# Stage openings of a 24-stage network kernel: remainders of the first PSUM bank ahead of units 3 and 4, for the lower token half too

## Chip, cores and metric

One core of a Trainium2 chip. The metric is device microseconds of one execution. A run's time is that of the whole program; three runs were taken.

## What is computed

Two blocks of four layers each on 256 tokens of width 1024 (float32, batch 1). The first block has, per layer, a gated FFN, a mixer (a spatial gate, dilated window attention or forgetting attention, each with attention over a memory) and a second FFN. The second has a mixer (block sparse attention, stick-breaking attention, a convolution, MoBA) and a squared-ReLU MLP per layer.

```
x = x + 0.5 * rms_norm(swiglu_ffn(rms_norm(x, g[0]), ...), g[1])
h = rms_norm(x, g[2])
y = mixer_a | mixer_b | mixer_c (h, rms_norm(mem), ...)
x = x + rms_norm(y, g[3])
x = x + 0.5 * rms_norm(swiglu_ffn(rms_norm(x, g[4]), ...), g[5])
...
x = x + mixer(_rms_norm(x, attn_norm[i]))
hm = _rms_norm(x, mlp_norm[i])
x = x + jnp.square(jax.nn.relu(hm @ mlp_w_up[i])) @ mlp_w_down[i]
```

Every stage thus starts with a norm of x and a product of the result with a weight matrix. Where these meet is what the change is about.

## The kernel before

**Stages.** The program is one list: four times ffn, mem_kv, mixer, ffn, then four times mixer (nsa, stick, conv, moba) and mlp. All but mem_kv begin with an *opening*, so there are 20. The 256 tokens are two halves of 128, lower (t = 0) and upper (t = 1).

**Products in three parts.** A float32 operand is written as a rounded part (hi) and the remainder (lo), and a product is hi*hi + hi*lo + lo*hi. In `half_chunk` on TensorE (PE) `hi_products` (L799, L800) multiplies the activations' hi with the weights' hi and lo, and `lo_product` (L803) the activations' remainder act_lo with the weights' hi.

**Weights.** They come in *units* of two 128-row tiles by up to 512 columns through a ring of 8 slots (SyncE issues the loads). Four units, numbered 0 to 3 here, make a chunk (K = 1024); units 4 to 7 are the next. ScalarE (ACT) copies a landed unit to ring_hi (L1402), then VectorE (DVE) subtracts it to get ring_lo (L1915, "split" below); the semaphores are hi_ready and lo_ready, in order of units. For stages that follow neither mem_kv nor the start, GpSimd (POOL) does the splits of units 5 and 7 (L2757, pool_lo_ready) instead. How far DVE splits ahead is given by the calls of `ahead(limit)` that are spread over its program.

**Activations.** In an opening PE transposes the normed rows nrm of a half, 8 tiles into two PSUM banks T0 and T1 (L775). DVE multiplies each bank with the gain into act_hi (L1929, two instructions of 128x512), then computes act_lo tile by tile (L1939, four instructions per bank, out = T * gain - act_hi); the last one of a bank raises t_taken of that bank. The generator `normed` holds these instructions, and the callers draw them with `next`: `start` for the lower half, in the midst of the residual of the stage before, and the stage's own code for the upper half. After `start` DVE updates x for the upper half of the previous stage (L2090 and L2093, or L2097), which its norm waits for.

**PE's order in an opening** (`opening`, `half_chunk` with lo_later): the first chunk takes the hi products first and the remainders later. Lower half: units 0 to 3, then a wait for both banks, then all eight remainder products. Upper half: units 0 and 1, a wait for bank 0, four remainder products, units 2 and 3, a wait for bank 1, the other four. Then follows the second chunk of the same half (units 4 to 7, all three parts together), and then the other half.

## Time and profile before

| | |
|---|---|
| runs | 3346.24 (median), 3345.96, 3359.56 us |
| profiled execution | 3356.01 us, its span 3354.3 us |
| PE matmul busy | 96% of the span |
| DVE busy | 58% |
| ACT busy | 49% |
| POOL busy | 6% |
| granted TensorE clock | 0.99 on average |
| chain that ended last | PE 86%, DVE 9%, ACT 3% |

The profile is of one execution. The span runs from the first to the last instruction. Busy shares are the union of an engine's instructions; PE's instructions overlap and their ends are modelled, so the start of each is what to go by. Idle time of an engine is put down to what released it. An instruction of DVE that has started also counts as busy while it waits for a port.

### The profile page before, as it was taken

The numbers are of one execution on the slowest core, as the hardware profiler recorded it, in microseconds if no ns is written. First come the engines' busy times: TensorE is split into PE (matmuls) and PEld (weight loads), VectorE is DVE, ScalarE is ACT, GpSimd is POOL, SyncE is SP. The second block draws the span as 40 slices with busy tenths as digits, with TensorE's granted clock in tenths as the row PEclk, the third lists the DMA queues.
The fourth block names the chain that finished last, engine by engine and source line by source line (L and its number), as shares of the span: only waits on it lengthen the run. The fifth ranks groups of instructions, "written<-read, shape, count | busy, mean of one in ns | idle before, by whom it ended". The sixth has DMA issues, their size and how long they took to land.

```text
span 3354.3 us, 52004 instructions
## 1 busy us (share of the span) xinstructions
PE 3227.4 (96%) x19601; PEld 2822.5 (84%) x19601; DVE 1933.2 (58%) x2856; ACT 1627.4 (49%) x2425; POOL 199.0 (6%) x258
## 2 busy tenths in 40 slices
PE   7999999998999999999999999899999999999999
PEld 7977988977998978897987897779788887887797
DVE  4656546565555654655556556565466566655663
ACT  4445445444444435544445445544354455545552
POOL 1001001000001000101000102000000000102100
PEclk9999999999999999999999999999999999999999
DMA  6653656642565643565554654435544550555364
GB/s 218 194 176 123 200 182 189 200 151 89 169 194 175 194 155 117 157 192 178 185 186 146 182 184 150 135 113 187 181 135 154 187 181 13 187 183 170 112 202 150
DMA packets 413278, 551.69 MB, mean 164 GB/s; under 512 B 33952, under 2 KB 263520, under 8 KB 413104
## 3 DMA queue, kind: packets, MB, share of 16 engines
q1 hardware_dynamic: 409248, 536.10, 49.8%
q0 software_dynamic: 2864, 10.38, 1.0%
q10 hardware_dynamic: 992, 2.84, 0.2%
q8 instruction: 114, 1.87, 0.2%
q14 instruction: 60, 0.49, 0.0%
HBM read 548.15 MB, written 1.05 MB: 164 GB/s over the span
## 4 chain that ended last, share of the span: by engine, by line
PE 86%; DVE 9%; ACT 3%; issue 1%; POOL 0%; DMA 0%; SPq 0%; DVEq 0%; ACTq 0%
PE G L799 15%; PE G L803 15%; PE G L800 15%; PE G L900 11%; PE G L901 11%; PE G L902 11%; DVE ring_lo_sb L1915 4%; PE T L775 2%; PE S L994 1%; PE O L1022 1%; DVE act_hi_sb L1929 1%; DVE act_lo_sb L1939 1%; PE G L1302 1%; ACT ring_hi_sb L1402 1%; DVE work_sb L2116 0%
## 5 line engine op out<-in xcount | busy, mean ns | idle before, releaser
L1915 DVE TENSOR_TENSOR ring_lo_sb<-ring_sb,ring_hi_sb 128x1024 fp32r<-128x1024 f32 (+1 forms) x998 | 1200.9, 1222 | 610.8 <-ACT ring_hi_sb L1402 592.4
L1402 ACT ACTIVATE ring_hi_sb<-ring_sb 128x1024 fp32r<-128x1024 f32 (+1 forms) x1028 | 1056.0, 1044 | 681.1 <-DMA ring_sb<-ffn_w_down 217.0
L900 PE MATMUL G<-act_hi_sb,ring_hi_sb 128*128 128x256 f32 x3136 | 877.1, 280 | 3.0 <-DVE ring_lo_sb L1915 3.0
L901 PE MATMUL G<-act_lo_sb,ring_hi_sb 128*128 128x256 f32 x3136 | 874.2, 279 | 0.0
L902 PE MATMUL G<-act_hi_sb,ring_lo_sb 128*128 128x256 f32 x3136 | 873.5, 279 | 0.0
L799 PE MATMUL G<-ring_hi_sb,hid_hi_sb 128*128 128x512 f32 x1456 | 582.5, 400 | 13.8 <-DVE hid_hi_sb L1948 6.5
L900 PEld LDWEIGHTS G<-act_hi_sb,ring_hi_sb 128*128 128x128 f32 x3136 | 589.5, 188 | 3.4 <-issue 3.2
L902 PEld LDWEIGHTS G<-act_hi_sb,ring_lo_sb 128*128 128x128 f32 x3136 | 589.1, 188 | 0.0
L901 PEld LDWEIGHTS G<-act_lo_sb,ring_hi_sb 128*128 128x128 f32 x3136 | 588.7, 188 | 0.0
L800 PE MATMUL G<-ring_lo_sb,hid_hi_sb 128*128 128x512 f32 x1456 | 578.5, 397 | 0.0
L803 PE MATMUL G<-ring_hi_sb,hid_lo_sb 128*128 128x512 f32 x1248 | 493.2, 395 | 0.0
L799 PE MATMUL G<-ring_hi_sb,act_hi_sb 128*128 128x512 f32 (+2 forms) x960 | 386.0, 402 | 36.2 <-DVE ring_lo_sb L1915 23.2
L800 PE MATMUL G<-ring_lo_sb,act_hi_sb 128*128 128x512 f32 (+2 forms) x960 | 371.5, 387 | 0.0
L799 PEld LDWEIGHTS G<-ring_hi_sb,hid_hi_sb 128*128 128x128 f32 x1456 | 275.3, 189 | 83.0 <-DVE hid_hi_sb L1948 8.2
L803 PE MATMUL G<-ring_hi_sb,act_lo_sb 128*128 128x512 f32 (+2 forms) x960 | 326.0, 383 | 8.7 <-DVE act_lo_sb L1939 8.7
L800 PEld LDWEIGHTS G<-ring_lo_sb,hid_hi_sb 128*128 128x128 f32 x1456 | 275.4, 189 | 65.1
L1988 DVE TENSOR_TENSOR work_sb<-G,work_sb 128x256 f32<-128x256 f32 (+1 forms) x240 | 117.1, 492 | 364.6 <-ACT work_sb L1453 364.6
L1453 ACT ACTIVATE work_sb<-G 128x256 f32<-128x256 f32 (+1 forms) x120 | 52.9, 441 | 513.6 <-PE G L902 412.3
L803 PEld LDWEIGHTS G<-ring_hi_sb,hid_lo_sb 128*128 128x128 f32 x1248 | 234.4, 188 | 57.7
L799 PEld LDWEIGHTS G<-ring_hi_sb,act_hi_sb 128*128 128x128 f32 x960 | 183.6, 191 | 99.4 <-DVE ring_lo_sb L1915 34.7
L803 PEld LDWEIGHTS G<-ring_hi_sb,act_lo_sb 128*128 128x128 f32 x960 | 179.9, 188 | 51.0 <-issue 13.6
L800 PEld LDWEIGHTS G<-ring_lo_sb,act_hi_sb 128*128 128x128 f32 x960 | 184.2, 192 | 34.0
(264 smaller groups left out, 2608.9 us busy)
## 6 DMA issues: line engine op xcount, KB each, us to landing
ring_sb<-ffn_w_gate_up SPq DMA_DIRECT2D x704, 256.0 KB, 3.9
ring_sb<-ffn_w_down SPq DMA_DIRECT2D x352, 256.0 KB, 3.7
ring_sb<-mlp_w_up SPq DMA_DIRECT2D x256, 256.0 KB, 3.6
ring_sb<-mlp_w_down SPq DMA_DIRECT2D x256, 256.0 KB, 3.7
ring_sb<-a_w_in SPq DMA_DIRECT2D x48, 256.0 KB, 4.3
ring_sb<-sb_w_in SPq DMA_DIRECT2D x48, 256.0 KB, 3.9
ring_sb<-moba_w_in SPq DMA_DIRECT2D x48, 256.0 KB, 4.1
ring_sb<-w_mem_kv SPq DMA_DIRECT2D x32, 256.0 KB, 3.8
```

The lines of the kernel that those rows point to most:

```text
L775: last = nc.tensor.transpose(bank[0:m, at:at + P], src, ident)
L799: mm(dst, lhs[0][:, kt, ts], ring_hi[:, slot, k, 0:w], start=start, stop=False)
L800: mm(dst, lhs[0][:, kt, ts], ring_lo[:, slot, k, 0:w], start=False, stop=False)
L803: return mm(dst, lhs[1][:, kt, ts], ring_hi[:, slot, k, 0:w], start=False, stop=stop)
L900: mm(dst, hi, act_hi[:, kt, :], start=(kt == 0 and f == 0), stop=False, skip_group_check=True)
L901: mm(dst, hi, act_lo[:, kt, :], start=False, stop=False, skip_group_check=True)
L902: last = mm(dst, lo, act_hi[:, kt, :], start=False, stop=(kt == KT - 1), skip_group_check=True)
L994: last = mm(S[:, t, 0:w], q, keys, start=(t == 0), stop=True, skip_group_check=True)
L1402: fn(ring_hi[:, s_, :, 0:w], ring[:, s_, :, 0:w], ACT.Copy).then_inc(hi_ready, 1)
L1453: fn(gated[:, par, 1, 0:w], G[:, 1, par, 0:w], f).then_inc(gated_ready, 1)
L1915: v.tensor_tensor(ring_lo[:, s_, :, 0:w], ring[:, s_, :, 0:w], ring_hi[:, s_, :, 0:w], ALU.subtract).then_inc(lo_ready, 1)
L1988: v.tensor_tensor(hid[:, par, t, 0:w], G[:, t, par, lo:lo + w], gated[:, par, t, 0:w], ALU.mult).then_inc(g_taken[t], 1)
```

## The change

For the lower half PE now does what it did for the upper one: after units 0 and 1 it waits for bank 0 and multiplies that bank's four remainders, and only then waits for unit 2's split and the second act_hi. On DVE the generator `normed` has one more stop, between the act_lo of bank 0 and that of bank 1. `start` draws act_hi and the act_lo of bank 0, then splits up to unit 3, then draws the act_lo of bank 1. All other callers draw three times in a row, which is the order they had. Line numbers of what follows move up by three for PE's part.

```diff
--- before.py
+++ after.py
@@ -818,13 +818,12 @@
                     return last
                 for u in range(CHUNK_UNITS):
                     slot = (n + u) % RING
+                    if lo_later and u == half:
+                        copied(c["T"] - 2)
+                        remainders(0, half)
+                        pe.wait_ge(act_hi_in, c["act_hi"])
                     if t == 0:
                         unit_split(n + u, step, i)
-                    if lo_later and u == half:
-                        if t == TT - 1:
-                            copied(c["T"] - 2)
-                            remainders(0, half)
-                        pe.wait_ge(act_hi_in, c["act_hi"])
                     for k in range(UNIT_K):
                         kt = UNIT_K * u + k
                         hi_products(dst, lhs, kt, ts, slot, k, width, kt == 0)
@@ -833,10 +832,8 @@
                     if t == TT - 1 and not lo_later:
                         last.then_inc(unit_used, 1)
                 if lo_later:
-                    if t == 0:
-                        copied(c["T"] - 2)
                     copied(c["T"] - 1)
-                    last = remainders(0 if t == 0 else half, CHUNK_UNITS)
+                    last = remainders(half, CHUNK_UNITS)
                 if t == 0:
                     last.then_inc(first_done, 1)
 
@@ -1932,6 +1929,8 @@
                             .then_inc(act_hi_in, 1)
                     yield
                     for b in range(2):
+                        if b:
+                            yield
                         n = c["T"]
                         dve.wait_ge(act_hi_in, c.up("act_hi"))
                         for j in range(4):
@@ -1956,8 +1955,8 @@
                 ahead(c["unit"] + CHUNK_UNITS)
                 if before is not None:
                     ahead(c["unit"] + RING)
-                    next(before)
-                    next(before)
+                    for _ in range(3):
+                        next(before)
                 for d, (c0, w) in enumerate(plan_):
                     c.up("unit", CHUNK_UNITS)
                     for t in range(TT):
@@ -2013,8 +2012,8 @@
                         split_one(n + d * CHUNK_UNITS + u, step, i)
 
                 ahead(n + RING)
-                next(before)
-                next(before)
+                for _ in range(3):
+                    next(before)
                 tb, turn0 = c["T"], c["turn"]
                 one(0, 0)
                 split_chunk(2)
@@ -2068,6 +2067,7 @@
                 if s < len(stages) and stages[s][0] != "mem_kv":
                     started[s] = normed(s)
                     next(started[s])
+                    next(started[s])
                     ahead(c["unit"] + CHUNK_UNITS)
                     next(started[s])
                 ahead(c["unit"] + CHUNK_UNITS + 1)
@@ -2146,8 +2146,8 @@
                 lead, cut, _ = quanta(kind)
                 before = started.pop(s)
                 ahead(n + RING)
-                next(before)
-                next(before)
+                for _ in range(3):
+                    next(before)
 
                 def take(d, t):
                     if t == 0:
@@ -2574,8 +2574,8 @@
                     done()
 
                 ahead(n + RING)
-                next(before)
-                next(before)
+                for _ in range(3):
+                    next(before)
                 tb = c["T"]
                 product(0, 0)
                 product(0, 1)
```

The stick stage's opening, lower half, on DVE: act_hi and act_lo are the activations' two parts, ring_lo a split, x_sb<-G the residual. Before:

```order
L1929 TENSOR_TENSOR act_hi_sb<-T,an_cols_sb 128x4x128 x2
L1915 TENSOR_TENSOR ring_lo_sb<-ring_sb,ring_hi_sb 128x1024 x2
L1939 SCALAR_TENSOR_TENSOR act_lo_sb<-T,an_cols_sb,act_hi_sb 128x128 x8
L1915 TENSOR_TENSOR ring_lo_sb<-ring_sb,ring_hi_sb 128x1024
L2097 TENSOR_TENSOR x_sb<-G,x_sb 128x1024
L1915 TENSOR_TENSOR ring_lo_sb<-ring_sb,ring_hi_sb 128x1024
```

With the change:

```order
L1926 TENSOR_TENSOR act_hi_sb<-T,an_cols_sb 128x4x128 x2
L1938 SCALAR_TENSOR_TENSOR act_lo_sb<-T,an_cols_sb,act_hi_sb 128x128 x4
L1912 TENSOR_TENSOR ring_lo_sb<-ring_sb,ring_hi_sb 128x1024 x2
L1938 SCALAR_TENSOR_TENSOR act_lo_sb<-T,an_cols_sb,act_hi_sb 128x128 x4
L1912 TENSOR_TENSOR ring_lo_sb<-ring_sb,ring_hi_sb 128x1024
L2097 TENSOR_TENSOR x_sb<-G,x_sb 128x1024
L1912 TENSOR_TENSOR ring_lo_sb<-ring_sb,ring_hi_sb 128x1024
```

The first four act_lo have moved ahead of the two splits (units 2 and 3). In the first opening and the four after mem_kv it is four and three splits, in the three ffn that follow an ffn and in nsa one, and in the other seven none.

The same opening on PE, from the first product on; t_taken0 and t_taken1 stand for the act_lo of the two banks. Before, from unit 2 on:

```order
L799 MATMUL G<-ring_hi_sb,act_hi_sb 128x512 [waits act_hi_in,lo_ready]
L800 MATMUL G<-ring_lo_sb,act_hi_sb 128x512
L799 MATMUL G<-ring_hi_sb,act_hi_sb 128x512
L800 MATMUL G<-ring_lo_sb,act_hi_sb 128x512
L799 MATMUL G<-ring_hi_sb,act_hi_sb 128x512 [waits lo_ready]
L800 MATMUL G<-ring_lo_sb,act_hi_sb 128x512
L799 MATMUL G<-ring_hi_sb,act_hi_sb 128x512
L800 MATMUL G<-ring_lo_sb,act_hi_sb 128x512
L803 MATMUL G<-ring_hi_sb,act_lo_sb 128x512 [waits t_taken1,t_taken0]
L803 MATMUL G<-ring_hi_sb,act_lo_sb 128x512 x7
```

With the change, from the end of unit 1 on:

```order
L803 MATMUL G<-ring_hi_sb,act_lo_sb 128x512 [waits t_taken0]
L803 MATMUL G<-ring_hi_sb,act_lo_sb 128x512 x3
L799 MATMUL G<-ring_hi_sb,act_hi_sb 128x512 [waits lo_ready,act_hi_in]
L800 MATMUL G<-ring_lo_sb,act_hi_sb 128x512
L799 MATMUL G<-ring_hi_sb,act_hi_sb 128x512
L800 MATMUL G<-ring_lo_sb,act_hi_sb 128x512
L799 MATMUL G<-ring_hi_sb,act_hi_sb 128x512 [waits lo_ready]
L800 MATMUL G<-ring_lo_sb,act_hi_sb 128x512
L799 MATMUL G<-ring_hi_sb,act_hi_sb 128x512
L800 MATMUL G<-ring_lo_sb,act_hi_sb 128x512
L803 MATMUL G<-ring_hi_sb,act_lo_sb 128x512 [waits t_taken1]
L803 MATMUL G<-ring_hi_sb,act_lo_sb 128x512 x3
```

The remainder products are now two groups of four, each with its own bank's wait, and the waits for unit 2 and for the second act_hi stand behind the first group.

## Rows read from the trace of the kernel before

**Rows 1.** Waits view: engine, line, releaser: us in total, times, longest.
```profile
PE G L799 <- DVE ring_lo_sb L1915: 23.2, 21, 2.8
PE G L803 <- DVE act_lo_sb L1939: 8.7, 9, 1.0
```

**Rows 2.** Timeline of DVE, stick opening: start us, us, instruction, count, [idle before].
```profile
2400.90 1.29 DVE L1929 TENSOR_TENSOR act_hi_sb<-T,an_cols_sb 128x512 fp32r<-128x512 f32 x2 [7.62 <-PE T L775]
2402.10 2.35 DVE L1915 TENSOR_TENSOR ring_lo_sb<-ring_sb,ring_hi_sb 128x1024 fp32r<-128x1024 f32 x2
2404.37 2.16 DVE L1939 SCALAR_TENSOR_TENSOR act_lo_sb<-T,an_cols_sb,act_hi_sb 128x128 fp32r<-128x128 f32 x8
2406.44 1.35 DVE L1915 TENSOR_TENSOR ring_lo_sb<-ring_sb,ring_hi_sb 128x1024 fp32r<-128x1024 f32 x1
2407.72 1.21 DVE L2097 TENSOR_TENSOR x_sb<-G,x_sb 128x1024 f32<-128x1024 f32 x1
2409.15 2.00 DVE L1915 TENSOR_TENSOR ring_lo_sb<-ring_sb,ring_hi_sb 128x1024 fp32r<-128x1024 f32 x1 [0.22 <-DVE x_sb L2097]
```

**Rows 3.** Timeline of PE, the same opening.
```profile
2401.64 0.50 PE L799 MATMUL G<-ring_hi_sb,act_hi_sb 128*128 128x512 f32 x1 [0.35 <-DVE act_hi_sb L1929]
...
2406.67 2.10 PE L803 MATMUL G<-ring_hi_sb,act_lo_sb 128*128 128x512 f32 x8 [0.97 <-DVE act_lo_sb L1939]
...
2414.21 1.04 PE L775 MATMUL T<-con_sb,nrm_sb 128*128 128x128 f32 x8
```

**Rows 4.** Timelines of ACT (two rows) and POOL (two), the same opening.
```profile
2402.86 1.06 ACT L1402 ACTIVATE ring_hi_sb<-ring_sb 128x1024 fp32r<-128x1024 f32 x1 [0.22 <-DMA ring_sb<-sb_w_in]
2411.87 1.15 ACT L1423 ACTIVATE nrm_sb<-x_sb,small_sb 128x1024 f32<-128x1024 f32 x1 [1.76 <-POOL small_sb L2718]
...
2403.99 2.72 POOL L2757 TENSOR_TENSOR ring_lo_sb<-ring_sb,ring_hi_sb 128x1024 fp32r<-128x1024 f32 x1 [8.62 <-ACT ring_hi_sb L1402]
2406.66 3.40 POOL L2757 TENSOR_TENSOR ring_lo_sb<-ring_sb,ring_hi_sb 128x1024 fp32r<-128x1024 f32 x1
```

**Rows 5.** Timelines of DVE (two rows) and POOL (one), opening of nsa.
```profile
2045.12 1.29 DVE L1929 TENSOR_TENSOR act_hi_sb<-T,an_cols_sb 128x512 fp32r<-128x512 f32 x2 [0.75 <-PE T L775]
...
2049.55 2.13 DVE L1915 TENSOR_TENSOR ring_lo_sb<-ring_sb,ring_hi_sb 128x1024 fp32r<-128x1024 f32 x1
...
2048.19 2.41 POOL L2757 TENSOR_TENSOR ring_lo_sb<-ring_sb,ring_hi_sb 128x1024 fp32r<-128x1024 f32 x1 [0.22 <-ACT ring_hi_sb L1402]
```

**Rows 6.** Timelines of DVE (two rows) and PE (one), opening after first mem_kv.
```profile
225.89 1.28 DVE L1929 TENSOR_TENSOR act_hi_sb<-T,pre_cols_sb 128x512 fp32r<-128x512 f32 x2
...
232.56 5.28 DVE L1915 TENSOR_TENSOR ring_lo_sb<-ring_sb,ring_hi_sb 128x1024 fp32r<-128x1024 f32 x4
...
232.79 0.70 PE L803 MATMUL G<-ring_hi_sb,act_lo_sb 128*128 128x512 f32 x2 [0.96 <-DVE act_lo_sb L1939]
```

**Rows 7.** Timeline of PE, the first opening.
```profile
14.31 0.77 PE L799 MATMUL G<-ring_hi_sb,act_hi_sb 128*128 128x512 f32 x1 [2.01 <-DVE ring_lo_sb L1915]
...
17.43 0.63 PE L800 MATMUL G<-ring_lo_sb,act_hi_sb 128*128 128x512 f32 x1
...
22.45 2.10 PE L803 MATMUL G<-ring_hi_sb,act_lo_sb 128*128 128x512 f32 x8 [0.96 <-DVE act_lo_sb L1939]
```

**Rows 8.** Timelines of DVE and POOL: first opening, then the moba stage.
```profile
12.95 2.35 DVE L1915 TENSOR_TENSOR ring_lo_sb<-ring_sb,ring_hi_sb 128x1024 fp32r<-128x1024 f32 x2
13.74 0.47 POOL L2711 TENSOR_SCALAR pool_tmp_sb<-sums_sb 128x1 f32<-128x1 f32 x1 [4.71 <-ACT nrm_sb L1413]
...
3062.46 0.42 DVE L2304 TENSOR_TENSOR head_tmp_sb<-proj_sb,tabs_sb 128x256 f32<-128x256 f32 x1
3061.70 1.27 POOL L2716 TENSOR_SCALAR head_rs_sb<-pool_neg_sb 128x4 f32<-128x4 f32 x1
```

**Rows 9.** Timelines of DVE and POOL, opening of conv.
```profile
2712.72 0.69 DVE L1929 TENSOR_TENSOR act_hi_sb<-T,an_cols_sb 128x512 fp32r<-128x512 f32 x1 [7.62 <-PE T L775]
2716.04 2.48 POOL L2757 TENSOR_TENSOR ring_lo_sb<-ring_sb,ring_hi_sb 128x1024 fp32r<-128x1024 f32 x1 [8.84 <-ACT ring_hi_sb L1402]
```

## Prediction

> **What bounds the kernel now.** I read the page's busy shares first: TensorE (PE) is busy for 96% of the span (the table above), VectorE (DVE) for 58%, so some 4% is left in which PE stands still. So a change in order can only pay where PE stands still, and the waits view says what ends those stretches. Two rows of it belong to the stage openings: 8.7 us, in nine waits, for the activation remainders (act_lo, L1939), and 23.2 us, in 21 waits, for weight remainders (ring_lo, L1915) [rows 1]. The first is what the change can remove; the second is what it can add to, since it moves act_lo ahead of ring_lo on DVE.
>
> Then I read one opening on each engine. Times from here on are counted from the start of the first act_hi write of the opening, 2400.90 in the stick stage. DVE: two act_hi writes, weight splits of units 2 and 3 from 1.20 to 3.55, eight act_lo from 3.47 to 5.63, split of unit 4 until 6.89, the x update (L2097) until 8.03, split of unit 6 from 8.25 to 10.25 [rows 2]. PE: first product at 0.74, remainders only at 5.77 after 0.97 idle, upper half's transposes at 13.31 [rows 3]. Between the last two lie 8 + 24 = 32 matmuls, so one is 0.235 us. POOL does units 5 and 7: the first starts at 3.09, 0.07 after ScalarE's (ACT) copy of unit 5 [rows 4].
>
> The third thing to see is in durations. A POOL split that meets nothing takes 2.4 [rows 5], a DVE split 1.2 (two in 2.35, rows 2). But POOL's first of this opening takes 2.72: it started while DVE was in the split of unit 3, and ended 2.26 after that one. DVE's split of unit 6 takes 2.00, and ends 1.09 after POOL's second [rows 2, 4]; in the nsa stage's opening DVE's split of unit 4 takes 2.13, and ends 1.08 after POOL's first [rows 5]. So a DVE split and a POOL split exclude each other, and the later waits for all that is left. The act_lo writes (one operand in PSUM) pass beside POOL at their usual 0.26 each.
>
> **The change, part by part.** There are 20 openings. Instructions are neither added nor removed. PE does four of its eight remainder products after unit 1; DVE does the four act_lo of bank 0 ahead of the splits up to unit 3. Every such split comes 4 x 0.26 = 1.04 later, what follows the eight act_lo keeps its place on DVE unless POOL shifts it.
>
> (a) Seven openings without a DVE split between act_hi and act_lo: DVE's order is the same, PE had no wait for act_lo. Nothing.
>
> (b) Four openings after mem_kv. POOL does no splits there. DVE goes through three splits and then act_lo; PE's remainders start at 232.79, which is 6.90 after zero, and end at 8.78 [rows 6]. Now: act_lo of bank 0 until 2.33, splits until 3.46, 4.60, 5.73, act_lo of bank 1 until 6.75 as before. PE: unit 0 from 0.74, unit 1 from 3.52, four remainders from 4.56, unit 2 from 5.5, unit 3 from 6.4, remainders from 7.4 to 8.3. Gain 0.48 each. In the first one DVE's four splits behind act_lo take 5.28 [rows 6] instead of the 4.6 of four undisturbed ones (the first is held until 8.55), and that takes 0.3 back: together 1.6. PE is the engine that all wait for until the upper half, so this reaches the end.
>
> (c) The very first opening. Splits 0 and 1 come 1.04 later, 2 and 3 wait for ACT's copies as before, act_lo ends 1.04 earlier. PE's eight remainders start at 22.45 and end at 24.3 [rows 7]; now the last four can start at 21.4. PE has units 0 and 1 a microsecond late, and they run at half speed there (eight products from 14.31 to 17.9, rows 7): unit 0 from 15.3, unit 1 from 17.1, four remainders from 18.9, unit 2 from 19.8, unit 3 from 20.7, remainders from 21.7 to 22.6. Gain 1.7.
>
> (d) Four openings with one DVE split in between (the three ffn that follow an ffn, and nsa). PE doesn't wait for act_lo there, but later, for DVE's split of unit 6 at the end of a gapless DVE chain (part of the 23.2 us in rows 1). So what PE has done earlier is of no use. That chain moves only where POOL's first split is asked for before DVE's of unit 3 has ended: in the nsa stage it started at 3.07 after zero [rows 5], now DVE's split lasts until 3.46. Loss 0.2 once.
>
> (e) Four openings with two DVE splits in between: stick, conv, moba, and the mlp after conv. Here the remainder wait is a full 0.97, and here DVE now has two splits back to back at 2.24 to 4.6, just where POOL asks for the port (3.09 in rows 4, between 2.7 and 3.3 in the others). Who gets it between the two? The trace has the case small. In the first opening POOL's one-column L2711 starts during the first of two back-to-back splits, and ends at 14.21, 0.13 after the second has begun (14.08): it was let in between them [rows 8]. Against that stands L2716 of the moba stage, which was let in only after the last of three rope products, and ended 0.09 after it [rows 8]; but those three have no semaphore wait between them, and splits do. I take the first. Then: split 2 until 3.46; POOL's first from 3.32 to 5.70; DVE's split 3 until 5.70 + 1.08 = 6.78; act_lo of bank 1 until 7.82; POOL's second until 6.78 + 2.27 = 9.05; split 4 until 10.13; x until 11.26; split 6 until 12.70. PE: unit 2 from 3.55 to 4.49; unit 3 from 6.84 to 7.88; remainders from 7.97 to 9.0; unit 4 from 10.19 to 11.7; unit 5 until 13.1, 6 and 7 until 15.9, where the transposes stood at 13.31. Loss 2.6. Late next would be the upper half's nrm: x at 11.26 instead of 8.03 makes it 15.4 at the latest (12.12 before, rows 4), still ahead of PE. In the conv stage POOL asks at 3.32 [rows 9], exactly at the hand-over; if DVE goes through, POOL's first ends at 6.83, split 4 at 7.91, split 6 at 11.26, PE's transposes at 14.2: loss 0.9. I take that one for conv.
>
> Sum: 3 x 2.6 + 0.9 + 0.2 - 1.6 - 1.7 = **+5.6 us**. The profiled execution took 3356.01 (span 3354.3), some 10 above the median of 3346.24 of the three runs, so I add the sum to the median: 3351.8.
>
> A rule bears on the one open point. By the trace the conv stage is a toss. The Trainium skill (SBUF — State Buffer, § Who interferes with whom) says that an operation of DVE with two SBUF inputs and one of GpSimd that reads SBUF exclude each other, and that whoever issues first has the port for its whole instruction. The durations of rows 2, 4 and 5 agree. By that rule POOL, which issues at 3.32 in conv against DVE's 3.37, would get it there too.
>
> **Rivals.**
> 1. POOL goes first in all four, the conv stage included: 1.7 more, 3353.5. For it: POOL's start at 3.32 is ahead of 3.37. Against: how long after its start it asks for the port no row shows. It is the outcome of the skill's rule above.
> 2. DVE keeps the port over both splits, as over the rope products: 4 x 0.9 + 0.2 - 3.3 = +0.5, 3346.7. For it the three rope products; against it L2711.
> 3. The port costs nothing new, because POOL is put off without harm: then (e) gains only 0.14 each, since split 6 at 10.25 holds PE 2.5 later: 4 x 0.14 + 3.3 = 3.9 less, 3342.4. Against: POOL's second split and split 6 follow each other in rows 2 and 4.
> 4. TensorE's clock falls in the new 2.35 us of idle at unit 3. After 2.0 idle, and a longer one before, the products from 14.31 on stand 0.43 to 0.45 apart instead of 0.235 [rows 7]; after shorter ones (0.97 in rows 3) they don't. At half speed until unit 4's work is through it would cost another 1.3 in each of three or four: 3355.7 to 3358.7.
> 5. **Slower than before by what can be measured**: POOL takes the port ahead of unit 3's split in the openings (d) as well, eight in all at 2.6: 20.8 - 3.3 = +17.5, 3363.7. It decides once POOL's first split starts before DVE's of unit 3 is through its predecessor, at 2.2; the earliest there is 3.07 [rows 5], as ACT's copy of unit 5 ends only then. Transfers would have to land 0.8 earlier.
> 6. The reordering does nothing that can be seen, gains and losses being swallowed by later waits: 3346.
>
> **How the numbers follow.** My case 0.35, rival 1 0.20, rival 2 0.20, rival 3 0.10, rival 4 0.08, rival 5 0.03, rival 6 0.04. A measurement of this kernel can tell about 0.5%, 16.7 us, from no change. All cases but rival 5 lie within that, so: faster 0.02 (rival 3 with what spread the runs have), same 0.93, slower 0.05 (rival 5, and rival 4 with that spread; one of the three runs shown is 13 above the others). The range goes from rival 3 to rival 4, 3341.5 to 3358.5. Its ends also hold the bounds of the two unknown prices: the port in (e), from 4 x 0.14 gained to 4 x 3.9 lost, and (c), from nothing to 1.9 gained.
>
> **What would show it.** In the changed profile: the nine waits of L803 for act_lo fall from 8.7 us to near nothing; in the stick, moba and post-conv mlp openings DVE's second split after the first four act_lo takes about 3.4 instead of 1.2, and PE has a new wait for ring_lo of about 2.3 there and one of 1.2 at unit 4, with the upper half's transposes at 15.9 after zero; in the nsa opening the wait for unit 6 is 0.2 longer. If DVE's two splits take 1.2 each there and POOL's first takes 3.7, rival 2 is right; if PE's products after the new idle are 0.43 apart, rival 4. The forecast is wrong in kind if those openings get shorter than before, or if the four openings after mem_kv don't.

## Result: 0.31% slower, and where it was lost

| | before | after |
|---|---|---|
| runs | 3358.80 us (median of 20) | 3369.84 us (median of 20) |
| lowest | 3345.96 | 3357.17 |
| ratio of after to before | | 1.0031, 95% interval 1.0020 to 1.0042 |
| profiled execution, its span | 3356.01, 3354.3 | 3369.36, 3367.6 |
| PE, DVE, ACT, POOL busy | 96, 58, 49, 6% | 96, 58, 48, 6% |

The ratio is worth +10.4 us (0.0031 x 3358.8), 6.7 to 14.1 by its interval. That is less than the 0.5% which the forecast took as the least that can be told from no change, but the interval lies wholly above 1. The forecast was +5.6 us, 3351.8, with a range up to 3358.5. One of the 20 runs of the changed kernel took 7944.59 us, for a reason that isn't known, and is left out of the ratio.

The waits view of the changed kernel, its three largest rows, the first of which answers to [rows 1] (engine, line, releaser: us in total, times, longest):

```profile
PE G L799 <- DVE ring_lo_sb L1912: 40.1, 30, 3.0
PE T L775 <- ACT nrm_sb L1420: 26.2, 6, 11.0
PE G L799 <- DVE act_hi_sb L1926: 12.5, 34, 0.5
```

There is no row for act_lo any more: the 8.7 us that the change went for are gone. But the wait for weight remainders has grown from 23.2 to 40.1 us. So 8.7 went and 16.9 came.

The stick opening on DVE, to be laid beside [rows 2] (start us, us, instruction, count, [idle before]); zero is 2400.35 here:

```profile
2400.35 1.29 DVE L1926 TENSOR_TENSOR act_hi_sb<-T,an_cols_sb 128x512 fp32r<-128x512 f32 x2 [7.61 <-PE T L775]
2401.56 1.12 DVE L1938 SCALAR_TENSOR_TENSOR act_lo_sb<-T,an_cols_sb,act_hi_sb 128x128 fp32r<-128x128 f32 x4
2402.59 4.54 DVE L1912 TENSOR_TENSOR ring_lo_sb<-ring_sb,ring_hi_sb 128x1024 fp32r<-128x1024 f32 x2
2407.05 1.12 DVE L1938 SCALAR_TENSOR_TENSOR act_lo_sb<-T,an_cols_sb,act_hi_sb 128x128 fp32r<-128x128 f32 x4
2408.09 2.35 DVE L1912 TENSOR_TENSOR ring_lo_sb<-ring_sb,ring_hi_sb 128x1024 fp32r<-128x1024 f32 x1
2410.37 1.21 DVE L2097 TENSOR_TENSOR x_sb<-G,x_sb 128x1024 f32<-128x1024 f32 x1
2411.80 1.23 DVE L1912 TENSOR_TENSOR ring_lo_sb<-ring_sb,ring_hi_sb 128x1024 fp32r<-128x1024 f32 x1 [0.22 <-DVE x_sb L2097]
```

Two weight splits in a row take 4.54 us where they took 2.35 [rows 2]. POOL's two run between 2403.40 and 2409.36:

```profile
2403.40 5.96 POOL L2757 TENSOR_TENSOR ring_lo_sb<-ring_sb,ring_hi_sb 128x1024 fp32r<-128x1024 f32 x2 [8.57 <-ACT ring_hi_sb L1399]
```

Taken singly, DVE's splits run 2.24 to 3.46 and 3.37 to 6.78 after zero, POOL's 3.05 to 5.69 and 5.65 to 9.01. So POOL was let in between DVE's two, DVE's second ended 1.09 after POOL's first, and POOL's second 2.23 after that one. PE in the same opening (to be laid beside [rows 3]):

```profile
2403.07 1.10 PE L803 MATMUL G<-ring_hi_sb,act_lo_sb 128*128 128x512 f32 x4
...
2407.19 0.50 PE L799 MATMUL G<-ring_hi_sb,act_hi_sb 128*128 128x512 f32 x1 [2.07 <-DVE ring_lo_sb L1912]
2407.52 0.58 PE L800 MATMUL G<-ring_lo_sb,act_hi_sb 128*128 128x512 f32 x1
2407.90 0.63 PE L799 MATMUL G<-ring_hi_sb,act_hi_sb 128*128 128x512 f32 x1
2408.33 0.63 PE L800 MATMUL G<-ring_lo_sb,act_hi_sb 128*128 128x512 f32 x1
2408.75 1.91 PE L803 MATMUL G<-ring_hi_sb,act_lo_sb 128*128 128x512 f32 x4
...
2416.45 1.03 PE L775 MATMUL T<-con_sb,nrm_sb 128*128 128x128 f32 x8
```

The remainders of bank 0 now run without idle time before them. After unit 2's products PE stands still until unit 3's split is there, at 6.84, and the upper half's transposes start at 16.09 after zero instead of 13.31.

That last number, the start of the upper half's transposes after zero, is the yardstick of all that follows, since it holds one opening and nothing else. It has a spread of its own: in the version below that changes (e) alone, the first opening, which that version leaves as it was, came 0.90 longer than before, and others came up to 0.99 shorter. So in single openings differences below 1 us count only where they come again in several versions, or where the rows show their cause. The 20 openings by the prediction's groups, after less before, in us:

| group | forecast | measured | single openings |
|---|---|---|---|
| (a) seven without a DVE split between | 0 | +1.85 | +1.29, +0.38, -0.04, +0.08, -0.14, +0.18, +0.10 |
| (b) four after mem_kv | -1.6 | -0.61 | +0.26, -0.58, -0.58, +0.29 |
| (c) first opening | -1.7 | -0.82 | |
| (d) three ffn after an ffn, nsa | +0.2 | +0.42 | +0.79, -0.32, -0.30, +0.25 |
| (e) stick, conv, mlp after conv, moba | +8.7 | +10.66 | +2.78, +2.64, +2.62, +2.62 |
| sum | +5.6 | +11.50 | |

The sum of +11.5 agrees with the +10.4 of the runs. The two spans differ by 13.3, so 1.8 lie outside the openings.

### The profile page after: what moved, and what is told of

It is laid out like the page before. It is cut to its first block, busy times and chain, and to the rows that moved or that the text cites. A ratio compares the mean times of both kernels' runs of the same rounds, so it can differ in the third digit from the quotient of the medians.

```text
span 3367.6 us, 51984 instructions
## 1 busy us (share of the span) xinstructions
PE 3231.8 (96%) x19601; PEld 2830.7 (84%) x19601; DVE 1945.0 (58%) x2856; ACT 1627.4 (48%) x2425; POOL 193.0 (6%) x258
## 4 chain that ended last, share of the span: by engine, by line
PE 86%; DVE 8%; ACT 3%; issue 1%; DMA 0%; POOL 0%; DVEq 0%; ACTq 0%; SPq 0%
PE G L799 16%; PE G L803 15%; PE G L800 15%; PE G L897 11%; PE G L898 11%; PE G L899 11%; DVE ring_lo_sb L1912 4%; PE T L775 2%; PE O L1019 1%; PE S L991 1%; DVE act_hi_sb L1926 1%; PE G L1299 1%; ACT ring_hi_sb L1399 1%; DVE act_lo_sb L1938 1%; DVE work_sb L2116 0%
## 5 line engine op out<-in xcount | busy, mean ns | idle before, releaser
L799 PE MATMUL G<-ring_hi_sb,act_hi_sb 128*128 128x512 f32 (+2 forms) x960 | 388.7, 405 | 52.8 <-DVE ring_lo_sb L1912 40.1
L803 PE MATMUL G<-ring_hi_sb,act_lo_sb 128*128 128x512 f32 (+2 forms) x960 | 333.1, 388 | 0.0
```

The lines of the kernel that those rows point to most:

```text
L799: mm(dst, lhs[0][:, kt, ts], ring_hi[:, slot, k, 0:w], start=start, stop=False)
L803: return mm(dst, lhs[1][:, kt, ts], ring_hi[:, slot, k, 0:w], start=False, stop=stop)
```

## Experiments

All ratios are against the kernel before, run on the same chip in turns. There were three such series on three chips, so compare ratios, not microseconds, between versions of different series; the medians of before in them were 3355.55, 3358.29 and 3357.31. Line numbers in the variants are up to 15 higher. Stages 18, 20, 21 and 22 of the program are those of (e). The variants share one addition: two sets of stages that say where DVE draws bank 0's act_lo early (NEW_DVE) and where PE takes bank 0's remainders early (NEW_PE).

```diff
--- after.py
+++ variants
+        NEW_DVE, NEW_PE = ..., ...
...
-                    if lo_later and u == half:
+                    early = lo_later and (t == TT - 1 or n in new_pe_units)
+                    if early and u == half:
                         copied(c["T"] - 2)
                         remainders(0, half)
+                    if lo_later and u == half:
                         pe.wait_ge(act_hi_in, c["act_hi"])
...
-                    next(started[s])
+                    if s in NEW_DVE:
+                        next(started[s])
                     ahead(c["unit"] + CHUNK_UNITS)
                     next(started[s])
+                    if s not in NEW_DVE:
+                        next(started[s])
```

### The change everywhere but in (e), and in (e) alone

```diff
+        NEW_DVE, NEW_PE = ALL - {18, 20, 21, 22}, ALL - {18, 20, 21, 22}
```

> The change everywhere but in the four openings with two splits (stick, conv, the mlp after conv, moba), which keep the old order on both engines. If the port hold-up in those four is the whole loss, their upper-half transposes stand at 13.3 us after the first act_hi again, and the kernel is 1 to 2 us faster than before (ratio 0.9995, not to be told from 1 by the times alone). If the loss is spread over other stages or comes from more half-clock stretches, the ratio stays above 1.001.

```diff
+        NEW_DVE, NEW_PE = {18, 20, 21, 22}, {18, 20, 21, 22}
```

> Only those four openings in the new order, all other 16 as before. Port theory: transposes at 15.95 to 16.1 in each (2.6 to 2.8 later), together +10.7 us, ratio 1.003. Spread theory: under half of that, ratio under 1.0015.

Without (e): 0.9992, interval 0.9976 to 1.0007, 3353.73 us. (e) alone: 1.0021, 1.0005 to 1.0037, 3362.91. So the loss is in (e), whose four openings stand at 13.31 to 13.51 again in the first version, and what the rest of the change gives can't be told from nothing.

In three of the four openings (e) alone costs +2.63, +2.64 and +2.63, as in the whole change. In moba it costs +0.92, and that one shows the mechanism from the other side. DVE and POOL there (zero is 3049.05):

```profile
3051.29 2.35 DVE L1920 TENSOR_TENSOR ring_lo_sb<-ring_sb,ring_hi_sb 128x1024 fp32r<-128x1024 f32 x2
3053.56 1.12 DVE L1946 SCALAR_TENSOR_TENSOR act_lo_sb<-T,an_cols_sb,act_hi_sb 128x128 fp32r<-128x128 f32 x4
3054.60 2.39 DVE L1920 TENSOR_TENSOR ring_lo_sb<-ring_sb,ring_hi_sb 128x1024 fp32r<-128x1024 f32 x1
...
3052.75 6.50 POOL L2768 TENSOR_TENSOR ring_lo_sb<-ring_sb,ring_hi_sb 128x1024 fp32r<-128x1024 f32 x2 [9.22 <-ACT ring_hi_sb L1407]
```

POOL's first split began at 3.70, behind DVE's second at 3.37, and DVE's two took their 2.35. POOL had to wait instead, its first took 3.16 (to 6.86), and what was held was DVE's split of unit 4 (2.39 instead of 1.2) and of unit 6. So DVE's order is the same in both cases, and POOL's start, 3.27 or earlier against 3.70, decides between 2.6 and 0.9.

### No POOL splits at all, in the new order and in the old

DVE splits every unit. First with the change everywhere, then in the old order.

```diff
-                by_pool |= {n + 5, n + 7}
+                by_pool |= set()
...
-                c.up("finished", 2)
+                c.up("finished", 0)
```

> The change, and DVE does the splits of units 5 and 7 as well, POOL none. Port theory: DVE's second split takes 1.2 again instead of 3.4, unit 3 no longer waits, transposes of the four openings within 0.3 us of those of the same kernel in the old order. Rival (the act_lo moved ahead cost the time by themselves, 1.04 us each, passed on through DVE's chain): transposes at least 1 us later than in the old order without POOL.

> The order before, POOL does no splits: the partner of the run above. DVE's chain gets two splits longer in the openings with POOL, so units 5 to 7 wait for it: in the four openings transposes at about 13.4, in those after an ffn later than before by about 1; by the times somewhat slower than before. Both theories expect the same of this one.

New order: 1.0009, 0.999 to 1.0027. Old order: 0.9996, 0.9982 to 1.0011. In (e) both have the transposes at 13.70, 14.00, 13.63 and 13.62 or 13.63, so **without POOL the new order costs nothing there**: of +2.6 each, all of it hangs on POOL's splits. What I expected of the old order was wrong for the ffn openings: I had them 1 us longer, and the openings of (d) became 0.64, 1.30, 0.95 and 0.42 shorter. So POOL's splits cost more there than they save. In (e) I had 13.4, and they came 0.31 to 0.68 longer than before.

### POOL held back until unit 3's split is done

The kernel is the changed one, and POOL waits in every opening in which it splits units.

```diff
+            if s in NEW_DVE:
+                hold_at[s] = n + CHUNK_UNITS - 1
...
+                if s in hold_at:
+                    pool.wait_ge(lo_ready, lo_no[hold_at[s]] + 1)
```

> The change, but POOL's first split waits (on lo_ready) until DVE has split unit 3, in every opening with POOL. Theory that the order of port requests decides: DVE goes through both splits, POOL's first runs from about 4.6 to 6.9, DVE's split of unit 4 ends at about 8, unit 6's at 11.3, transposes of stick, conv, post-conv mlp and moba at 14.2 (0.9 later than before, not 2.6); the whole at +2 to +3 us against before (ratio 1.0008). If what POOL takes from DVE costs the same wherever it falls, they stay at 15.9.

3363.23, 1.0020, 1.0005 to 1.0036. The stick opening:

```profile
2402.85 2.35 DVE L1922 TENSOR_TENSOR ring_lo_sb<-ring_sb,ring_hi_sb 128x1024 fp32r<-128x1024 f32 x2
2405.11 1.12 DVE L1948 SCALAR_TENSOR_TENSOR act_lo_sb<-T,an_cols_sb,act_hi_sb 128x128 fp32r<-128x128 f32 x4
2406.15 2.60 DVE L1922 TENSOR_TENSOR ring_lo_sb<-ring_sb,ring_hi_sb 128x1024 fp32r<-128x1024 f32 x1
2408.68 1.21 DVE L2110 TENSOR_TENSOR x_sb<-G,x_sb 128x1024 f32<-128x1024 f32 x1
2410.11 1.98 DVE L1922 TENSOR_TENSOR ring_lo_sb<-ring_sb,ring_hi_sb 128x1024 fp32r<-128x1024 f32 x1 [0.22 <-DVE x_sb L2110]
```

With the one intrusion taken away, DVE's two splits are back at 2.35 and the four openings lose 1.13, 1.13, 1.14 and 1.15 instead of 2.6. I had expected 0.9, the price of moba above; POOL starts at 4.67, 0.08 after the split that it waits for, its first ends at 7.07 instead of 6.86, and DVE's split of unit 4 at 8.15 instead of 7.94: the missing 0.2. POOL's work was free at neither place tried: put later, it holds the splits of units 4 and 6.

The whole lost more than the 2 to 3 us that I had expected (the ratio is worth +6.7). Besides the 4.55 of (e), two single openings stand out by the yardstick. One ffn after an ffn lost 2.20: POOL's first split began there at 4.36 and ran to 7.91, its second held DVE's split of unit 6 until 12.30, and PE had slow products behind 2.72 of idle time. One opening after mem_kv lost 0.97 to slow products alone:

```profile
707.48 0.56 PE L805 MATMUL G<-ring_hi_sb,act_hi_sb 128*128 128x512 f32 x1 [1.57 <-DVE ring_lo_sb L1922]
707.84 0.63 PE L806 MATMUL G<-ring_lo_sb,act_hi_sb 128*128 128x512 f32 x1
708.26 0.63 PE L805 MATMUL G<-ring_hi_sb,act_hi_sb 128*128 128x512 f32 x1
```

The granted clock was 0.54 from 707.5 to 711.0. In the changed kernel the same opening has the same 1.57 of idle time and no slow products behind it.

### PE's new order alone, DVE's new order alone

```diff
+        NEW_DVE, NEW_PE = set(), ALL
```

> PE in the new order, DVE in the old (splits up to unit 3 first, then act_lo of both banks). Chain theory: PE waits after unit 1 for bank 0, which DVE delivers at 4.6 (four openings with two splits) or 5.7 (after mem_kv): transposes 0.8 later than before in these eight and in the first opening, nothing in the others; +7 us, ratio 1.002. Rival (the early wait is hidden, since PE catches up where it waited for act_lo before): within 0.2 us of before everywhere.

```diff
+        NEW_DVE, NEW_PE = ALL, set()
```

> DVE in the new order everywhere (act_lo of bank 0 ahead of the splits up to unit 3), TensorE's products in the order of before (hi products of units 0 to 3, then one wait for both banks, then all eight remainders). If the loss sits in DVE's two back-to-back splits and POOL's going between them, it is all here: in stick, conv, the mlp after conv and moba DVE's second split takes 3.4 us, split of unit 4 ends at 10.1, and the upper half's transposes stand at 15.9 to 16.1 after zero instead of 13.31, +2.6 each. After mem_kv nothing can be gained, since the eight remainders still wait for the last act_lo, which comes no earlier: 0 in each, where the whole change gained 0.58 in two. Rival: part of the 2.6 comes from TensorE's new order (units 2 and 3 behind four remainders); then (e) loses clearly less than 2.6 here. Sum +10.6 to +12, ratio 1.003 to 1.004, that is, as the whole change.

PE alone: 1.0053, 1.0032 to 1.0073 (some +18 us where +7 was expected). DVE alone: 1.0037, 1.0021 to 1.0052. Each half by itself is slow, and both cost more than the order of work explains. DVE alone came at the total that I had expected, 1.0037, but by a different sum: (e) lost 13.7 instead of 10.6, one opening after mem_kv lost 0.96 where I had 0 (seven slow products behind 1.56 of idle time), another 0.29, and the first gained 1.75. What the order doesn't explain is TensorE's clock. DVE alone, stick opening (zero 2395.80), PE:

```profile
2402.63 0.80 PE L803 MATMUL G<-ring_hi_sb,act_hi_sb 128*128 128x512 f32 x1 [2.06 <-DVE ring_lo_sb L1920]
2403.22 0.63 PE L804 MATMUL G<-ring_lo_sb,act_hi_sb 128*128 128x512 f32 x1
2403.65 0.63 PE L803 MATMUL G<-ring_hi_sb,act_hi_sb 128*128 128x512 f32 x1
2404.07 0.63 PE L804 MATMUL G<-ring_lo_sb,act_hi_sb 128*128 128x512 f32 x1
2404.50 3.62 PE L807 MATMUL G<-ring_hi_sb,act_lo_sb 128*128 128x512 f32 x8
```

Stretches of the same opening (window, length, PE busy and count, granted clock, DMA share, GB/s):

```profile
2396.50:2402.50 6.00, 3.29 (x12) 0.93 0.45 166
2402.70:2408.30 5.60, 5.60 (x13) 0.50 0.00 0
2408.50:2413.70 5.20, 5.20 (x24) 1.00 0.00 0
```

After the 2.06 of idle time the clock stood at 0.50, which is 1.2 GHz, over 13 products 0.43 apart, and at 2.4 GHz again behind them. The transposes stand at 17.99, 4.68 later than before. In conv it is +4.77, in the mlp after conv +3.35 with fewer slow products. In moba POOL asked at 3.39 and DVE's second split had begun at 3.37: DVE kept the port, its two splits took 2.35, and the opening lost 0.94. With only PE in the new order, idle time of over 2 us stands in the four openings after mem_kv, with slow products behind it, and these lose 2.29, 2.19, 2.21 and 3.51; the first opening, with 3.26 idle and slow products behind it, loses 3.19. At full speed the order would cost 0.8: the first remainder at 5.87 after zero and 40 products of 0.235 make 15.27, against 14.45. In (e) it costs 0.77. The waits view of that version has the act_lo wait at more than twice what it was:

```profile
PE G L807 <- DVE act_lo_sb L1946: 21.4, 13, 3.3
```

In the changed kernel itself the slow clock is there too, behind the 2.07 of idle time in two of the four openings (the rows 0.43 apart above, granted clock 0.55 from 2407.2 to 2410.6). It costs next to nothing there: only eight products lie between the wait for unit 3 and that for unit 4's split, which ends at 10.09 in any case. With slow products the transposes stand at 16.09 and 15.94, in the two others, without them, at 15.96 and 15.94. The idle time before was the same, 2.07 and 2.06 with slow products, 2.08 and 2.06 without. Conv's rows:

```profile
2722.44 0.50 PE L799 MATMUL G<-ring_hi_sb,act_hi_sb 128*128 128x512 f32 x1 [2.08 <-DVE ring_lo_sb L1912]
2722.78 0.39 PE L800 MATMUL G<-ring_lo_sb,act_hi_sb 128*128 128x512 f32 x1
```

So the length of the idle time doesn't say by itself whether slow products follow.

### The wait made two, and POOL only where it pays

The gain that was expected can be sought without moving anything on DVE. Here both engines keep the order of before, and the one wait for both banks is made two, so that the first four remainder products start when bank 0 is done. The edit is shown against the kernel before.

```diff
-                    if t == 0:
-                        copied(c["T"] - 2)
-                    copied(c["T"] - 1)
-                    last = remainders(0 if t == 0 else half, CHUNK_UNITS)
+                    if t == 0:
+                        copied(c["T"] - 2)
+                        remainders(0, half)
+                    copied(c["T"] - 1)
+                    last = remainders(half, CHUNK_UNITS)
```

> Nothing moved on DVE and no product moved on PE; only the one wait for both banks ahead of the eight remainder products is made two, bank 1's behind the first four. Theory: PE's wait of 0.96 shrinks to 0.2 in the nine openings that had it; of this 0.8 each arrives in the first opening and after the mem_kv of mix_b and mix_c, less in the two mix_a openings (POOL's affine select), and 0.15 each in the four with two splits, where unit 6's split is the next bound: 3 to 4 us faster, ratio 0.999, no opening later than before. Rival: PE's remainders run into unit 4's split everywhere and nothing is gained.

Then POOL's splits in the four openings of (e) only, with the two waits and without them:

```diff
-            if s and kind != "mem_kv" and stages[s - 1][0] != "mem_kv":
+            if s in (18, 20, 21, 22):
                 by_pool |= {n + 5, n + 7}
...
-                if stages[s][0] == "mem_kv":
+                if s not in (18, 20, 21, 22):
```

> Two waits as in the run before, and POOL splits units 5 and 7 only in the four openings with two DVE splits (where it is worth 0.3 to 0.7 each by the runs without POOL); elsewhere DVE does them, which by those runs is worth 0.65 to 1.3 in the openings of ffn after ffn and nsa, and 0.2 to 0.4 in the mlp ones. Expected 6 to 8 us faster than before, ratio 0.998. If without POOL the times don't fall here either, the ratio is that of the run before.

> The kernel before with one edit: POOL splits units 5 and 7 only in the four openings of stick, conv, the mlp after conv and moba; in all others DVE does them, as it already does at the start and after mem_kv. From the runs without any POOL splits I expect the openings of the three ffn that follow an ffn to be 0.65, 1.3 and 0.95 us shorter, nsa 0.4, the mlp after nsa 0.3, the last mlp 0.2, and the four here named as before (they were 0.3 to 0.7 longer without POOL): 3.8 us less, ratio 0.9989. The rival is that the version that had this edit and the two waits owed its gain to the two waits (some 1.7 us after mem_kv, given back in part by the mix_a openings); then this one is at 1.000.

The version with both, run once more:

> The same program as e9_two_waits_pool4, run once more, since its interval came close to 1: order of before on both engines, the one wait for both banks made two, POOL's splits only in the four openings. If its gain was no luck, it is again below 1: expected from its openings -0.6, -0.7, -1.3, -1.0, -1.0, -0.4, -0.3, -0.6, -0.2, 4 x -0.1 and +0.5 in one mix_a opening and +0.2 in the first, some -5.8 us, ratio 0.9983. If the two waits' rival holds (no gain outside of the spread), 1.000.

| version | us, median | ratio | interval |
|---|---|---|---|
| two waits | 3357.60 | 1.0002 | 0.9988 to 1.0017 |
| POOL in four openings | 3352.26 | 0.9984 | 0.9970 to 0.9998 |
| both | 3350.45 | 0.9984 | 0.9969 to 0.9999 |
| both, again | 3345.82 | 0.9973 | 0.9958 to 0.9988 |

The kernel before had 3358.29 beside the first and the third row, 3357.31 beside the two others.

The two waits alone can't be told from before, where I had expected 3 to 4 us; in the profiled execution the openings of (a), which this version doesn't touch in order, came 2.7 longer. Their act_lo waits are gone, but in (e) that is worth only 0.09 to 0.10 each, since the split of unit 6 holds PE next; the two openings after mem_kv without a spatial gate gain 0.74 and 1.00, and the other two lose 0.50 and 0.51, where POOL's affine select (see below) came at 6.47 and 6.51 after zero instead of 5.91 and 4.62. POOL in four openings alone gains: (d) is 0.63, 1.29, 0.95 and 0.41 shorter, as expected to 0.02; three of (e) are as before, and moba is 1.10 longer, since POOL's first split came at 4.65 in that execution. The rival, that the gain was the two waits' alone, falls: the interval of POOL in four openings clears 1 only just, but (d) came shorter by the same amounts, within 0.02, in all five versions in which POOL leaves these openings alone. Both together beat the kernel before, and with it the changed one, in two series of runs. That the two waits add to POOL's share is likely by the single openings (0.74 and 1.00 after mem_kv, 0.1 in each of (e)), but the intervals overlap.

```profile
PE G L803 <- DVE ring_lo_sb L1921: 25.0, 29, 2.8
```

This is the waits row of the last version: the wait for weight remainders is 25.0 us where it was 23.2, and the 8.7 for act_lo have no row.

## Why the prediction came out as it did

**What held.** (e), the port. POOL let in between two splits of DVE: DVE's second split 3.4 long (forecast until 6.78, measured 6.78), split 4 until 10.09 (10.13), split 6 until 12.67 (12.70), transposes at 15.94 to 16.09 (15.9), +2.6 each (+2.62 to +2.78). The nine waits for act_lo fell to nothing; nsa lost 0.25 (0.2). (e) alone and the two versions without POOL show that this is the cause. Rival 5, the whole of (d) lost as well, did not happen, and rival 3 fell with (e) itself.

**What failed, by its step.** The measured 3369.84 lies 18.0 above the forecast of 3351.8. Of that, 12.6 is the base of the sum (step 5), and it alone puts the result outside the range; the other 5.4 is the sum, +5.6 forecast against +11.0 between the medians (+10.4 by the ratio, +11.5 in the openings; steps 1 to 4).

1. *(e), the toss in conv.* I took the small loss of 0.9 there; it was 2.64. POOL asked at 3.27 against DVE's 3.37 and was let in, which is rival 1, the outcome of the rule named there. 1.7 us.

2. *(b), the gain of 0.48 each.* The two without a spatial gate gained 0.58. The first and the last lost 0.26 and 0.29, so (b) gave 0.6 instead of 1.6. POOL's affine select (L2745) reads SBUF for 1.56 us when it meets nothing, and starts when its transfer lands. In the first one it starts at the same time as before, 231.80, 6.24 after zero; in the last it comes much later than before:

```profile
231.80 1.56 POOL L2745 TENSOR_SCALAR_AFFINE_SELECT spat_w_sb<-spat_w_sb 128x1536 f32<-128x1536 f32 x1 [8.69 <-DMA spat_w_sb<-a_spatial_t]
...
1771.69 2.21 POOL L2745 TENSOR_SCALAR_AFFINE_SELECT spat_w_sb<-spat_w_sb 128x1536 f32<-128x1536 f32 x1 [9.55 <-DMA spat_w_sb<-a_spatial_t]
```

In both it holds DVE's splits: the four behind act_lo take 5.61 and 5.98 where four undisturbed ones take 4.62. For the first I had counted 0.3 from the 5.28 of [rows 6]. But the transfer lands at a time of its own (231.81 before, 231.80 now) while the opening starts 0.33 earlier (225.56 instead of 225.89), so the hold reaches that much deeper into it. In the last one it stood before at 4.62 after zero, where it met nothing, and now at 7.09; I had not looked there. This time moves between executions without the change too: in the two versions that leave both openings untouched, (e) alone and POOL in four openings, it was 6.02 and 6.21 in the first, 5.56 and 5.75 in the last. So how much of the 0.26 and 0.29 is the change's own isn't shown.

```profile
232.23 5.61 DVE L1912 TENSOR_TENSOR ring_lo_sb<-ring_sb,ring_hi_sb 128x1024 fp32r<-128x1024 f32 x4
...
715.69 4.62 DVE L1912 TENSOR_TENSOR ring_lo_sb<-ring_sb,ring_hi_sb 128x1024 fp32r<-128x1024 f32 x4
...
1771.27 5.98 DVE L1912 TENSOR_TENSOR ring_lo_sb<-ring_sb,ring_hi_sb 128x1024 fp32r<-128x1024 f32 x4
```

In the version with the change everywhere but in (e) the select of the first came at 5.77, and the opening gained 0.20, near the 0.18 that I had worked out; the last lost 0.09.

3. *(c), the gain of 1.7.* It was 0.82. I had counted full speed for the four remainders from 18.9 on. PE's rows show them at half speed too:

```profile
16.00 0.77 PE L799 MATMUL G<-ring_hi_sb,act_hi_sb 128*128 128x512 f32 x1 [3.04 <-DVE ring_lo_sb L1912]
...
19.56 1.91 PE L803 MATMUL G<-ring_hi_sb,act_lo_sb 128*128 128x512 f32 x4
21.26 0.58 PE L799 MATMUL G<-ring_hi_sb,act_hi_sb 128*128 128x512 f32 x1
```

The first product stands where I had it (3.78 after zero, forecast 3.74), and so do the remainders (7.33). Then twelve products are 0.43 apart, until 21.26, where before it were eight [rows 7]: four more by 0.2 are the 0.8 that is missing. With DVE's new order alone the same opening gained 1.75, with the slow stretch over at 7.6 after zero, 19.4. How long the stretch lasts there changes with the execution: in the version with (e) alone changed, this untouched opening had a second slow stretch, behind its next idle time of 1.45, from 7.95 to 12.33 after zero, and was 0.90 longer than before.

4. *(a) and (d), nothing and 0.2.* DVE's order is unchanged in (a). The +1.29 of one ffn opening is slow products from its start until 5.1 after zero instead of until about 2, and such stretches come and go with the execution: with (e) alone changed, three of these untouched openings differed from before by +0.31, +0.53 and -0.99. The +0.79 of one opening in (d) is the port again: POOL's second split came at 7.43 instead of 6.64, inside DVE's x update (L2093), which took 2.88 instead of 2.32. That too is not the change's doing: with (e) alone changed, this opening is untouched, POOL's second split came at 7.36, and the opening was 0.73 longer.

5. *The base of the sum, the largest miss.* I put the sum on the median of three runs, 3346.24. Twenty runs of the same kernel had a median of 3358.8, and the profiled execution of 3356.01 was an ordinary one. By that the forecast would have been 3361.6. As a ratio the range reached from -0.14 to +0.37%, which holds +0.31; as an absolute time, 3358.5 at most, it doesn't hold 3369.84. Put on 3358.8, the same range would run from 3354.1 to 3371.1, and hold it. That the ratio lies inside is in part luck: (e) cost 1.9 more than its term, and (a), with 1.85 where I had nothing, is the spread of slow products.

The slow clock (rival 4) was right as a mechanism and wrong as a price: in the changed kernel it fell behind two of the four new idle stretches and cost 0 to 0.15, and it cost 0.7 to 2.1 each (16.67 to 18.09 against 15.9) where twelve products instead of eight followed with no other wait behind them (DVE's new order alone). The prediction tied it to idle time of 2.0, by rows 7, against 0.97 in rows 3; 2.06 and 2.08 without it and 1.57 with it show that the length alone doesn't decide.

**Open.** The same kernel before runs from 3343.90 to 3368.31 over all series. In the traces two parts of that can be seen: whole ffn stages whose 864 products of 256 columns step by 0.114 or by 0.118 us on average (98.8 or 102.2 us per stage), and slow stretches after idle time or at the start of an opening. What sets either from one execution to the next isn't known. Nor was it tried what would happen if DVE's two splits had no wait between them.

## What to carry to other kernels

Before moving an instruction ahead of a pair that shares a port with another engine, write down when that other engine asks: a request that now falls between two back-to-back instructions can change which of them goes first and cost far more than the move gains, here 2.6 us for 0.97 of wait removed. When the two requests lie within some tenths of a microsecond, take both outcomes into the sum. A wait at the end of a group is often worth splitting in two before anything is moved; but count what it will really give, since here most of it was taken by the next wait. Help from a second engine on the same port can cost more than it saves: POOL's splits were worth 0.3 to 0.7 us in each of the four openings of (e), and cost 0.2 to 1.3 in seven of the eleven others. Put a worked-out sum on a base of the size of run that it comes from, not on a median of three.

## What the runs showed of the hardware

- DVE and POOL at the port, two back-to-back splits of DVE with the second starting at 3.37: ten POOL splits that started at 2.52 to 3.27 after zero went between them; those that started at 3.39 and 3.70 did not. Two more requests fell just ahead of a single DVE split (unit 4). In the first pair of rows (DVE's new order alone) POOL began 0.10 ahead and had the port, and DVE's split took 3.38. In the second (POOL held back) it began 0.05 ahead, and DVE's split took 1.21, so DVE had it. So by the recorded starts the switch lies between 0.10 and 0.05 ahead of DVE's.

```profile
1030.52 2.40 POOL L2768 TENSOR_TENSOR ring_lo_sb<-ring_sb,ring_hi_sb 128x1024 fp32r<-128x1024 f32 x1 [2.32 <-ACT ring_hi_sb L1407]
1030.62 3.38 DVE L1920 TENSOR_TENSOR ring_lo_sb<-ring_sb,ring_hi_sb 128x1024 fp32r<-128x1024 f32 x1
...
1562.25 6.85 POOL L2772 TENSOR_TENSOR ring_lo_sb<-ring_sb,ring_hi_sb 128x1024 fp32r<-128x1024 f32 x2 [2.37 <-ACT ring_hi_sb L1409]
1562.30 1.21 DVE L1922 TENSOR_TENSOR ring_lo_sb<-ring_sb,ring_hi_sb 128x1024 fp32r<-128x1024 f32 x1
```

  The Trainium skill (SBUF — State Buffer, § Who interferes with whom) says that the order of issue decides which of the two blocks. The starts here agree with it down to 0.10 us; the request that began 0.05 ahead and had to wait shows how far a recorded start can be trusted as that order.
- A held instruction ends a constant time after the one that held it: DVE's split 1.08 to 1.09, POOL's 2.23 to 2.29.
- Slow stretches of TensorE: products 0.43 apart instead of 0.235, the granted clock at 0.50, that is 1.2 GHz. They stood behind idle time of 2.0 to 3.3 us in many openings, but also behind 1.56 or 1.57 in three openings after mem_kv (of POOL held back, of DVE's new order alone, of the new order without POOL), and at the start of ffn openings. There were none behind 2.06 and 2.08 in moba and conv of the changed kernel, none behind 1.57 in its openings after mem_kv, and none behind the 0.97 of rows 3. The traces don't show what decides it. What had hidden it in two cases was another wait due a few products later.
